# A two-layer hybrid decoder trunk on one Trainium2 core: the delta rule's prelude in another order

## The reference

```python
conv = causal_conv(qkv, w)                     # four taps per channel, then SiLU
q, k = l2_norm(q), l2_norm(k)                  # x * rsqrt(sum(x*x) + EPS)
q = to_chunks(q) * (dk ** -0.5)
g = jnp.cumsum(g, axis=-1)
diff = g[..., :, None] - g[..., None, :]
decay = jnp.where(tril, jnp.exp(jnp.where(tril, diff, 0.0)), 0.0)
k_beta, v_beta = k * beta[..., None], v * beta[..., None]
a_low = jnp.where(strict, jnp.einsum('bhnid,bhnjd->bhnij', k_beta, k) * decay, 0.0)
t_mat = a_low + jnp.eye(L)
u = lax.linalg.triangular_solve(t_mat, v_beta, ...)
w = lax.linalg.triangular_solve(t_mat, k_beta * jnp.exp(g)[..., None], ...)
qk = jnp.einsum('bhnid,bhnjd->bhnij', q, k) * decay
k_dec = k * jnp.exp(g_last[..., None] - g)[..., None]
q_dec = q * jnp.exp(g)[..., None]
def step(state, inp):                          # over the four chunks
    v_new = u_i - w_i @ state
    o = q_i @ state + qk_i @ v_new
    state = state * exp(g_last) + k_dec.T @ v_new
```

## Time and profile before

| | |
|---|---|
| median of 3 runs | 2024.49 us (2017.31 to 2025.18) |
| the profiled execution's own time | 2042.03 us |
| its span, from first to last instruction | 2040.1 us |
| mean granted TensorE clock in it | 0.955 |
| PE busy | 1917.3 us (94%) |
| DVE busy | 1304.4 us (64%) |
| ACT busy | 922.4 us (45%) |
| POOL busy | 229.5 us (11%) |

### The profile page before, as it was taken

How to read it: one execution, slowest core, us unless ns; L and a number is a source line. 1 busy time by engine, 2 the same in 40 slices (tenths; PEclk the granted TensorE clock), 3 DMA queues, 4 the chain that set the end, 5 groups by cost and what they waited for, 6 DMA issues and landing times.

```text
span 2040.1 us, 21737 instructions
## 1 busy us (share of the span) xinstructions
PE 1917.3 (94%) x8775; PEld 1345.6 (66%) x8775; DVE 1304.4 (64%) x1515; ACT 922.4 (45%) x1058; POOL 229.5 (11%) x224
## 2 busy tenths in 40 slices
PE   6999997998899999999989978999999999999996
PEld 5444855645588864457565456878788787878784
DVE  4597257221355537952651224988989898989895
ACT  4221144113444412302430144777777777777774
POOL 8470002001000046400020001000000000000010
PEclk7999998689999999999995997999999999999998
DMA  7333422026455244333310335999999999999992
GB/s 229 124 124 124 165 83 83 1 81 218 160 190 191 75 145 163 124 124 124 124 43 1 134 134 195 393 375 389 359 373 377 360 395 357 391 361 391 348 395 104
DMA packets 206451, 434.80 MB, mean 213 GB/s; under 512 B 8600, under 2 KB 47872, under 8 KB 206352
## 3 DMA queue, kind: packets, MB, share of 16 engines
q1 hardware_dynamic: 196464, 414.20, 56.0%
q0 software_dynamic: 5072, 16.90, 2.3%
q10 hardware_dynamic: 4816, 2.34, 0.4%
HBM read 422.93 MB, written 10.49 MB: 212 GB/s over the span
## 4 chain that ended last, share of the span: by engine, by line
PE 82%; DVE 10%; ACT 3%; issue 2%; DMA 1%; ACTq 1%; POOL 0%; DVEq 0%; SPq 0%
PE bank L2022 22%; PE bank L2422 13%; PE bank L2424 13%; PE bank L2423 13%; PE bank L2015 6%; DVE split_e L1326 3%; PE bank L2221 2%; DVE phase L1536 1%; ACT split_e L874 1%; PE bank L2329 1%; PE bank L2087 1%; PE bank L2556 1%; PE bank L2328 1%; PE bank L2315 1%; DMA ring<-in_moe_w_up 1%
## 5 line engine op out<-in xcount | busy, mean ns | idle before, releaser
L1326 DVE TENSOR_TENSOR split_e<-ring,split_e 128x2048 fp32r<-128x2048 f32 x264 | 600.2, 2288 | 54.6 <-ACT split_e L874 54.5
L874 ACT ACTIVATE split_e<-ring 128x2048 fp32r<-128x2048 f32 x264 | 503.8, 1919 | 160.7 <-PE bank L2424 155.1
L2022 PE MATMUL bank<-ring,hT 128*128 128x512 f32 x768 | 337.5, 597 | 1.7 <-ACT hT L1116 1.7
L2422 PE MATMUL bank<-split_e,fx_e 128*128 128x512 f32 x704 | 279.3, 397 | 2.0 <-DVE fx_e L1876 2.0
L2424 PE MATMUL bank<-split_e,fx_e 128*128 128x512 f32 x704 | 275.4, 391 | 0.0
L2423 PE MATMUL bank<-split_e,fx_e 128*128 128x512 f32 x704 | 274.9, 390 | 0.0
L2022 PEld LDWEIGHTS bank<-ring,hT 128*128 128x128 f32 x768 | 144.4, 191 | 179.8 <-issue 177.7
L2422 PEld LDWEIGHTS bank<-split_e,fx_e 128*128 128x128 f32 x704 | 132.7, 188 | 28.3 <-DVE fx_e L1876 2.2
L2424 PEld LDWEIGHTS bank<-split_e,fx_e 128*128 128x128 f32 x704 | 132.6, 188 | 28.3
L2423 PEld LDWEIGHTS bank<-split_e,fx_e 128*128 128x128 f32 x704 | 132.7, 188 | 26.4
L2422 PE MATMUL bank<-split_e,f_actT_e 128*128 128x512 f32 x352 | 138.7, 394 | 9.6 <-DVE f_actT_e L1884 9.6
(11 more groups left out here) (450 smaller groups left out, 2677.9 us busy)
## 6 DMA issues: line engine op xcount, KB each, us to landing
ring<-in_moe_w_gate SPq DMA_DIRECT2D x40, 2048.0 KB, 11.8
ring<-in_moe_w_up SPq DMA_DIRECT2D x40, 2048.0 KB, 11.5
ring<-in_moe_w_down SPq DMA_DIRECT2D x40, 2048.0 KB, 12.0
ring<-in_w_in SPq DMA_DIRECT2D x28, 2048.0 KB, 7.8
ring<-in_ffn_w_gate SPq DMA_DIRECT2D x11, 1024.0 KB, 5.6
ring<-in_ffn_w_up SPq DMA_DIRECT2D x11, 1024.0 KB, 8.2
ring<-in_ffn_w_down SPq DMA_DIRECT2D x11, 1024.0 KB, 8.8
ring<-in_ssm_w_glu SPq DMA_DIRECT2D x8, 1024.0 KB, 6.2
```

Of the source, the lines that this page charges most:

```text
L874: nc.scalar.activation(split_e[j % NBUF][:, HI, :], ring[:, s * PIECE + i * HGRP:s * PIECE + (i + 1) * HGRP], ACT.Copy).then_inc(split_hi, 1)
L1326: V.tensor_tensor(split_e[j % NBUF][:, LO, :], ring[:, s * PIECE + i * HGRP:s * PIECE + (i + 1) * HGRP], split_e[j % NBUF][:, HI, :].bitca ...
L2022: last = mm(B[bank][:, :], src[:, k, t * P:(t + 1) * P], w[:, k, n0:n0 + 512], start=k == 0, stop=k == kt - 1)
L2422: mm(bank, a[HI], w[HI], start=first, stop=False)
```

## The change

No operation is added; every product, scaling and exponential is still made, on the same engine and of the same size, but for one pair of masks on `decT`, which become one operation of twice the width. What moves:

* DVE makes the decay steps directly after the third piece of the attention branch, and SiLU of q and k before v's taps. The cumulative sum's matmul stands ahead of the first `memory_keys` and goes to `B[3]`.
* ACT makes `conv_tanh` of q and k before v's first tap, and of v after the decay exponentials. k's norm factors come before q's.
* The decay rows come before the second `memory_keys`, into `B[0]` and `B[1]`.
* k's scaling precedes q's; k's transposes and Gram product precede q's Gram product and v's transposes. The Gram products have banks of their own (6 and 7), so they no longer wait for k's evacuation.
* DVE makes `A_low` and `vbeta` first. The mask of `decT` and `qkT` are made beside level 0, `kbeg` and `kdec` beside level 1, q's scaling beside level 2, and the output gate beside levels 3 and 4 (`beside_level`).

Temporary buffers move accordingly. In the fences on the order, line numbers of the changed kernel differ from those before by a few lines.

The diff, cut to its core:

```diff
-        rq = [kbeg, vbeta, kdec, qkT_buf]
+        rq = [flat(v)[:, j * 512:(j + 1) * 512] for v in (kbeg, vbeta) for j in range(2)]
...
+        silu_tmp = [halves[i] for i in (3, 5, 2)]
+        square_tmp = [halves[i][:, j * 512:(j + 1) * 512] for i in (4, 0) for j in range(2)]
...
+                conv_tanh(0)
+                conv_tanh(1)
                 act.wait_ge(up_ps, 8 * l + 4)
                 first_taps(range(8, 12))
-                for i in range(3):
-                    conv_tanh(i)
                 for i in range(4):
                     act.wait_ge(cv_ready, 3 * l + i // 2 + 1)
-                    tmp = halves[3 + i // 2][:, (i % 2) * 512:(i % 2 + 1) * 512]
-                    nc.scalar.activation(tmp, cv[:, 2 * i:2 * i + 2, :].rearrange("p c n -> p (c n)"),
+                    nc.scalar.activation(square_tmp[i], cv[:, 2 * i:2 * i + 2, :].rearrange("p c n -> p (c n)"),
...
-                    r_ = rq[i].rearrange("p t h n -> p (t h n)")[:, 0:512]
+                for i in (2, 3, 0, 1):
...
+                act.wait_ge(dec_in, NT * (l + 1))
                 for t in range(NT):
-                    act.wait_ge(dec_in, NT * l + t + 1)
-                    nc.scalar.activation(e_row[:, t], B[2 + t][:, :].rearrange("p (h n) -> p h n", h=GH),
+                    nc.scalar.activation(dec[:, t], Dcl[:, t], ACT.Exp, scale=-1.0).then_inc(dec_ready, 1)
+                for t in range(NT):
+                    nc.scalar.activation(e_row[:, t], B[t][:, :].rearrange("p (h n) -> p h n", h=GH),
                                          ACT.Exp).then_inc(dec_ready, 1)
-                    nc.scalar.activation(dec[:, t], Dcl[:, t], ACT.Exp, scale=-1.0).then_inc(dec_ready, 1)
                     nc.scalar.activation(decT[:, t], DTm[:, t], ACT.Exp).then_inc(dec_ready, 1)
-
+                conv_tanh(2)
...
+                def decay_steps():
+                    dve.wait_ge(g_ln, l + 1)
+                    link(V.scalar_tensor_tensor(gate_z, gate_z, 0.0, gate_e, ALU.max, ALU.add))
+                    for t in range(NT):
+                        last = V.scalar_tensor_tensor(gstep.rearrange("p (t h) -> p t h", t=NT)[:, t, :], z4[:, t, :],
+                                                      -1.0, ealog, ALU.mult, ALU.mult)
+                    last.then_inc(g_step, 1)
+                    dve.wait_ge(gate_tanh, 2 * l + 1)
+                    V.tensor_scalar(beta, beta, 0.5, 0.5, ALU.mult, ALU.add)
+
+                def silu(i):
+                    dve.wait_ge(cv_th, 3 * l + i + 1)
+                    c4 = cv[:, 4 * i:4 * i + 4, :].rearrange("p c n -> p (c n)")
+                    V.scalar_tensor_tensor(c4, silu_tmp[i], 1.0, c4, ALU.add, ALU.mult).then_inc(cv_ready, 1)
+
                 for i in range(4):
                     if i > 0:
                         taps(i, range(8))
                     moba_branch(i)
...
+                    if i == 2:
+                        decay_steps()
+                silu(0)
+                silu(1)
...
+                for w in range(1, 4):
+                    taps(w, range(8, 12))
...
+                for n, i in enumerate((2, 3, 0, 1)):
+                    dve.wait_ge(cv_rs, 4 * l + n + 1)
+                    r_ = rq[i]
+                    c2 = cv[:, 2 * i:2 * i + 2, :].rearrange("p c n -> p (c n)")
+                    V.scalar_tensor_tensor(c2, r_, GD ** -0.5 if i < 2 else 1.0, c2, ALU.mult, ALU.mult).then_inc(kq_ready, 1)
+                silu(2)
...
+                dve.wait_ge(kk_ps, 2 * l + 1)
+                dve.wait_ge(dec_ready, 3 * NT * l + NT)
+                link(V.tensor_tensor(heads(A_low), B[6][:, :].rearrange("p (h n) -> p h n", n=GL), heads(dec), ALU.mult))
+                V.tensor_tensor(heads(A_low), heads(A_low), be2, ALU.mult).then_inc(a_ready, 1)
...
+                def beside_level(k):
+                    if k == 0:
+                        dve.wait_ge(dec_ready, 3 * NT * (l + 1))
+                        link(V.tensor_tensor(heads(decT), heads(decT), causal2[:, :].unsqueeze(1).to_broadcast([P, NT * GH, GL]),
+                                             ALU.mult))
+                        dve.wait_ge(kk_ps, 2 * l + 2)
+                        V.tensor_tensor(heads(qkT), B[7][:, :].rearrange("p (h n) -> p h n", n=GL), heads(decT),
+                                        ALU.mult).then_inc(qk_ready, 1)
+                    if k == 1:
+                        for t in range(NT):
+                            dve.wait_ge(kv_evac, NT * l + t + 1)
+                            V.tensor_tensor(kbeg[:, t], k_tok[:, t], per_token(bx3, t), ALU.mult)
+                            V.tensor_tensor(kdec[:, t], k_tok[:, t],
+                                            decT[:, t, :, GL - 1].unsqueeze(2).to_broadcast([P, GH, GD]), ALU.mult)
+                    if k == 2:
+                        for t in range(NT):
+                            qc = cv[:, 0:4, t * P:(t + 1) * P]
+                            V.tensor_tensor(qc, qc, e_row[:, t], ALU.mult).then_inc(qd_ready, 1)
+                    if k == 3:
+                        dve.wait_ge(gate_tanh, 2 * l + 2)
+                        V.scalar_tensor_tensor(gz, gz, 1.0, z_tok[:, :, :].rearrange("p t (h n) -> p (t h) n", h=GH),
+                                               ALU.add, ALU.mult)
+                    if k == 4:
+                        V.scalar_tensor_tensor(gz, gz, 0.5, gnorm_bc[:, l, :].unsqueeze(1).to_broadcast([P, NT * GH, GD]),
+                                               ALU.mult, ALU.mult)
 
...
+                    beside_level(k)
...
+                pe.wait_ge(ms_exp, MH * (l + 1))
+                pe.wait_ge(g_step, l + 1)
+                mm(B[3][:, 0:NT * GH], cum_mask[:, :], gstep, start=True, stop=True).then_inc(gc_ps, 1)
                 pe.wait_ge(memn_ready, KD * (l + 1))
-                pe.wait_ge(ms_exp, MH * (l + 1))
                 arrived(l, U_WK)
                 memory_keys(0, 2)
 
-                pe.wait_ge(up_used, 8 * l + 4)
-                pe.wait_ge(g_step, l + 1)
-                mm(B[1][:, 0:NT * GH], cum_mask[:, :], gstep, start=True, stop=True).then_inc(gc_ps, 1)
                 for i in range(4):
                     pe.wait_ge(cv_sq, 4 * l + i + 1)
-                    tmp = halves[3 + i // 2][:, (i % 2) * 512:(i % 2 + 1) * 512]
-                    mm(B[4 + i][:, :], ones[:, :], tmp, start=True, stop=True).then_inc(cv_ss, 1)
-                memory_keys(1, 0)
-                pe.wait_ge(xk_sb, 6 * l + 1)
+                    mm(B[4 + i][:, :], ones[:, :], square_tmp[i], start=True, stop=True).then_inc(cv_ss, 1)
+                pe.wait_ge(up_used, 8 * l + 4)
                 for t in range(NT):
                     pe.wait_ge(g_diag, NT * l + t + 1)
-                    mm(B[2 + t][:, :], ones[:, :], gdiag[:, t].rearrange("p h n -> p (h n)"), start=True,
+                    mm(B[t][:, :], ones[:, :], gdiag[:, t].rearrange("p h n -> p (h n)"), start=True,
                        stop=True).then_inc(row_ps, 1)
-
-                pe.wait_ge(kq_ready, 4 * (l + 1))
+                pe.wait_ge(gc_sb, l + 1)
+                memory_keys(1, 3)
+
+                pe.wait_ge(cv_rs, 4 * (l + 1))
+                pe.wait_ge(kq_ready, 4 * l + 2)
...
-                pe.wait_ge(kv_evac, NT * (l + 1))
-                for a, bank in ((4, 4), (0, 5)):
+                for a, bank in ((4, 6), (0, 7)):
+                    if a == 0:
+                        pe.wait_ge(kq_ready, 4 * (l + 1))
...
+                pe.wait_ge(cv_ready, 3 * (l + 1))
+                for t in range(NT):
+                    pe.wait_ge(kv_evac, NT * l + t + 1)
+                    for h in range(GH):
+                        last = tr(B[4 + t][:, h * P:(h + 1) * P], cv[:, 8 + h, t * P:(t + 1) * P], ident[:, :])
+                    last.then_inc(kv_ps, 1)
...
-                            pe.wait_ge(qk_ready, l + 1)
...
+                pe.wait_ge(qk_ready, l + 1)
+                pe.wait_ge(qd_ready, NT * (l + 1))
```

72 lines of the change are left out of this document (12 added, 60 removed).

## The result

| | before | after |
|---|---|---|
| median, same chip (us) | 2024.84 | 1996.07 (1981.79 to 1998.18) |
| ratio after/before | | 0.9861 [0.9819, 0.9904] |
| profiled execution, own time / span (us) | 2042.03 / 2040.1 | 1998.18 / 1996.4 |
| its mean granted clock | 0.955 | 0.970 |
| first level, from the layer's up-projection (us; layer 0 / 1) | 51.27 / 51.15 | 39.08 / 39.08 |

The forecast was 2000.0, its range 1989 to 2010. All times "from the up-projection" are differences of two starts: that of the first 128x512 product of the input projection in the layer (layer 1: 994.42 before, 963.50 after) and that of the first product of the named step; the levels end where the first transform behind them starts. To put a time of before on layer 1's clock of after, take 30.92 off.

The account below looks back on a forecast made before the run. The prediction took a serial chain in each layer's prelude, with PE idle and at a low clock, as the bound. 11.3 + 1.0 = 12.3 us per layer, 24.6 in both, off 2024.5 gave 1999.9, say 2000; range 1989 to 2010.

Parts of the forecast that it names:

- The path up to the first level: Layer's prelude: with the work reordered, PE's first level starts at 1034.3 instead of 1045.57, 11.3 us earlier per layer.
- The first level: First of the levels: 4.8 us long instead of 5.83, POOL's second mask 0.55 late; gains 1.0 us per layer.
- The scalings in DVE's idle time: Levels: moved scalings fit into DVE's 2.71 us of idle time per level, so they are hidden.
- the predicted 0.6 of overrun: Level 1: four scalings, two lengthened by masks, take 3.3 us, 0.6 over DVE's idle time; taken as hidden.
- Sum: Whole kernel: 11.3 + 1.0 = 12.3 us per layer, 24.6 in both, taken off the median 2024.5.
- What was carried unchanged: Whole kernel: the profiled execution lies 17.5 us above the median of the runs shown; this difference was assumed to stay.
- DVE and ACT late: Rival, 12%: before the first level, A_low behind v's SiLU becomes the bound; 9 us gained per layer, 2006.5.
- The shared port: Rival, 9%: level 1's four DVE products each wait out a whole POOL mask; 3.7 us per layer lost, 2007.3.
- the 0.98 of the sum: Levels: time in us assumed for a DVE product of two SBUF operands beside POOL's masks, against 0.68 otherwise.
- the 1.61 of the rival: Level 1: time in us of a DVE product that waits out a whole mask, 0.68 + 0.93; rival's chance 9%.
- Gain given back: Rival, 4%: a later transfer sets the pace and the earlier levels only wait for it; 2024.
- Clock falls in the levels: Rival, 5%: PE drops to 1.2 GHz in the levels, a level takes up to 8.5 us; 2050.7, slower.

Follow-up runs that it names:

- e9: Changed kernel with everything made beside the levels put back on DVE ahead of the first subtraction, behind vbeta; 2002.12 us (one run).
- e10: Changed kernel with kbeg and kdec made one level earlier, so that level 0 has six operations beside it; 2004.55 us (one run).
- e1: Kernel before with only DVE's queue reordered: A_low first, vbeta next, five scalings beside the levels, prelude kept; 2004.03 us, ratio 0.9923.
- e2: Changed kernel with v's transposes put back ahead of both Gram products; 2004.96 us (one run).
- e5: Changed kernel again, without an edit, for more runs beside the kernel before; 1996.78 us, ratio 0.9856.
- e7: Changed kernel with v's twelve taps put back ahead of the SiLU of q and k; 2007.25 us (one run).
- e11: Changed kernel with the decay rows on PE put back behind the second memory_keys and the sums of squares; 2023.19 us (one run).
- e3: Changed kernel with one memory-values fill product moved into PE's 0.76 us gap ahead of the chunk steps, later fills moved up; 1978.65 us, ratio 0.9782.
- e4: Kernel before with one memory-values fill product moved into the gap ahead of the chunk steps, later fills moved up; 2008.88 us, ratio 0.9938.
- e8: e3 with the last five memory-values products all made directly behind the chunk steps; 1983.20 us, ratio 0.9803.
- e6: Changed kernel with no memory-values fill in the first chunk step and two in the second; 1989.86 us, ratio 0.983.

## Why the prediction held, step by step

**The path up to the first level.** Forecast for the sum of the decays, on after's clock (forecast less 30.92): 978.8; measured 978.82. Sums of squares 986.5 and 986.02; decay rows 990.0 and 989.45; second fill 991.9 and 991.17; k's transposes 999.0 and 998.08; POOL 1002.7 and 1001.80; PE's first level 1003.4 and 1002.58. The order of releases is the one I gave; the 0.8 to 0.9 us come in small pieces, because the first product took 0.36 for 0.56 and the records of two steps in a row overlap by some 0.16 (986.02 + 3.60 is 989.62, the next begins at 989.45), while I put their lengths end to end. The gain there was 12.1, not 11.3.

**The first level.** Term 1.0, measured 1.5: 4.33 us instead of the 4.8 of the sum. I had the second mask 0.55 late. It was not: before, DVE's products of two SBUF operands stood beside the masks and stretched them too (twelve in 11.13; the second took 1.17), after only one of the twelve is stretched (8.72; the second took 0.73). I had read the earlier trace rows for what POOL does to DVE and not for the reverse.

**The scalings in DVE's idle time.** Right that they are hidden, by another way: the masks end 0.5 us before the first of the four, so these take 0.69 and the predicted 0.6 of overrun never arises. Had they met, 0.98 would have been too low; e9 and e10 show 1.2. The trace of before had it too: the 1.97 of the earlier trace rows are one product of 0.84, which began ahead of the first stretched mask, and one of 1.21. I had taken their mean. And the one product that did meet the masks, the mask of `decT`, stood in the sum with 0.68 and took 1.06.

**Sum.** 12.3 per layer forecast, 13.6 measured; 24.6 and 27.2 in both. With 27.2 off the 2024.5 I'd have said 1997.3, within 1.3 us of the median.

**What was carried unchanged.** The 17.5 us between the profiled execution and the median I took off without a name. By the groups it is one layer's chunk steps at 1.2 GHz: 43.9 against 25.6. That it could be carried through is luck: both medians happen to fall into the middle group.

**The rivals.** DVE and ACT late: no; v's SiLU has ended 0.76 before `A_low` begins. The shared port: not met by the four products of level 1; only L1625 met it, hidden in idle time. e9 and e10 met it, 1.2 per product, between the 0.98 of the sum and the 1.61 of the rival. The Trainium skill, "SBUF — State Buffer", section "Who interferes with whom", has the two engines exclude each other for a whole instruction: the direction agrees, on both engines, and the size nearly does, as 1.13 us hold one of each where strict turns would be some 1.3. Gain given back: no, the later stages moved as a block. Clock falls in the levels: no, 1.00 from 1005 to 1030. I had looked for the clock's risk in the levels; it was right behind them, and already there before.

**The pause at the hand-over.** The two layers of the kernel after show the same gap with two outcomes, layer 0 first:

```profile
363.71 1.08 PE L2327 MATMUL bank<-phase,uT 64*64 64x128 f32 x8 [0.76 <-ACT phase L1093]
...
1030.83 1.29 PE L2327 MATMUL bank<-phase,uT 64*64 64x128 f32 x8 [0.76 <-ACT phase L1093]
```

With the gap filled, the slower groups are missing from 13 runs. The profiles say the same: in the nine with the gap (before, after, e1, e2, e5, e7, e9, e10, e11) the chunk steps were cold in 10 of 18 layers, and in each of the ten the granted clock fell 0.6 to 1.4 us after the first chunk product had started; in the three with the gap filled (e3, e4, e8) none of 6 layers was cold. So the gap is part of the cause, or the large product in its place is part of the cure: no run tells these apart. What decides between the two outcomes stays open. The Trainium skill, "TensorE: Matmul & The Clock Gate", section "What's actually happening", ties the half clock to idleness. The fall agrees with it in direction; that PE then stays at 1.2 GHz for some 41 us while busy all the time (1031.6 to 1072.5) does not.

## What to carry to other kernels

When an idle engine waits for a chain, look at what the engine that feeds the chain does first: moving work that is not on the chain behind it gave 13.6 us per layer here, and a part of it through the clock that PE keeps. Compare stages of two profiles, not their spans: 16.5 of the 43.7 us between these two profiles were not the change. And try to fill even a pause of 0.76 us ahead of a stage of small products: at the hand-over one moved product was worth another 18 us in the median (e5 against e3, on two chips) and took the scatter from 31 us to 3.

## What was not expected of the hardware

- A stage of small products, PE busy throughout, ran at 1.2 GHz for nearly its whole length or at 2.4 GHz, 43.3 or 25.6 us; the clock fell at its start or not at all.
- During four 128x512 records in a row the clock rose from 0.50 to 1.00 in the middle of such a stage (e6).
- A DVE product of two SBUF operands beside a GpSimd mask lengthens both: 0.68 to 1.21 and 0.72 to 1.17 us, in step at one of each per 1.13. DVE operations that read a PSUM bank took 0.69 both beside the masks and without them.
